# A hybrid diffusion step on one core: recurrence with two numerators, four changes of order, and weighted values on VectorE

## The reference

```python
def step(carry, inp):
    C, n, m = carry
    qb, kb, vb, ib, fb = inp
    bcum = jnp.cumsum(fb, axis=-1)
    ...
    w_inter = jnp.exp(a - m_t)
    Wd = jnp.exp(Dm - m_t[..., None])
    s = jnp.einsum('bhtd,bhsd->bhts', qb, kb) * Wd
    num = w_inter[..., None] * jnp.einsum('bhtd,bhde->bhte', qb, C) + jnp.einsum('bhts,bhse->bhte', s, vb)
    den = w_inter * jnp.einsum('bhtd,bhd->bht', qb, n) + jnp.sum(s, axis=-1)
    h = num / jnp.maximum(jnp.abs(den), jnp.exp(-m_t))[..., None]
    w_last = Wd[..., -1, :]
    wi_last = w_inter[..., -1]
    C_new = wi_last[..., None, None] * C + jnp.einsum('bhs,bhsd,bhse->bhde', w_last, kb, vb)
```

## Time and profile before

| | before |
|---|---|
| median of 3 runs | 2494.33 us (2493.68 to 2495.67) |
| the profiled execution | 2489.8 us, of which the span of the core's instructions is 2488.0 |
| TensorE busy | 2420.6 us, 97% of the span, 14856 matmuls |
| VectorE busy | 1769.2 us, 71% |
| ScalarE busy | 909.0 us, 37% |
| GpSimd busy | 347.4 us, 14% |
| DMA | 289.76 MB, 116 GB/s on the mean |
| mean granted TensorE clock | 0.996 of full speed |

### The profile page before, as it was taken

How to read it: one execution, slowest core, us unless ns; L and a number is a source line. 1 busy time by engine, 2 the same in 40 slices (tenths; PEclk the granted TensorE clock), 3 DMA queues, 4 the chain that set the end, 5 groups by cost and what they waited for, 6 DMA issues and landing times. The chain is left out here.

```text
span 2488.0 us, 38914 instructions
## 1 busy us (share of the span) xinstructions
PE 2420.6 (97%) x14856; PEld 2227.7 (90%) x14856; DVE 1769.2 (71%) x2701; ACT 909.0 (37%) x1745; POOL 347.4 (14%) x373
## 2 busy tenths in 40 slices
PE   6999999999999899999999999999999999999998
PEld 5998999789989789979988998899899979989997
DVE  4887588858454769887855988786567559856863
ACT  4211121343343554423435442343421154423432
POOL 0000000110121421202202220121200021201211
PEclk9999999999999999999999999999999999999999
DMA  6544455435222323263342326333244323243332
GB/s 241 161 143 134 129 152 163 134 111 148 72 57 73 93 98 94 64 218 100 86 154 81 88 68 212 102 86 124 80 144 136 104 83 103 69 149 98 86 125 95
DMA packets 359638, 289.76 MB, mean 116 GB/s; under 512 B 38918, under 2 KB 317334, under 8 KB 358454
## 3 DMA queue, kind: packets, MB, share of 16 engines
q1 hardware_dynamic: 359478, 287.59, 38.2%
HBM read 275.32 MB, written 12.18 MB: 116 GB/s over the span
## 5 line engine op out<-in xcount | busy, mean ns | idle before, releaser
L2031 DVE TENSOR_TENSOR w_lo<-w_raw,w_hi 128x512 fp32r<-128x512 f32 (+2 forms) x287 | 259.4, 905 | 295.9 <-ACT w_hi L1445 292.9
L1445 ACT ACTIVATE w_hi<-w_raw 128x512 fp32r<-128x512 f32 (+2 forms) x287 | 228.9, 800 | 603.4 <-PE psum L1035 213.3
L960 PE MATMUL psum<-w_hi,act_hi 128*128 128x512 f32 x800 | 319.4, 399 | 8.9 <-DVE w_lo L2031 8.7
L962 PE MATMUL psum<-w_hi,act_lo 128*128 128x512 f32 x800 | 317.2, 396 | 0.0
L961 PE MATMUL psum<-w_lo,act_hi 128*128 128x512 f32 x800 | 317.0, 396 | 0.0
L1035 PE MATMUL psum<-hT_hi,w_hi 128*128 128x320 f32 x1216 | 278.3, 310 | 0.6 <-DVE w_lo L2031 0.5
L1035 PE MATMUL psum<-hT_hi,w_lo 128*128 128x320 f32 x1216 | 277.1, 309 | 0.0
L1035 PE MATMUL psum<-hT_lo,w_hi 128*128 128x320 f32 x1216 | 276.9, 309 | 0.0
L1079 PE MATMUL psum<-hT_hi,w_hi 128*128 128x320 f32 x684 | 211.6, 309 | 1.6 <-DVE z_quarters L2314 1.6
L1080 PE MATMUL psum<-hT_lo,w_hi 128*128 128x320 f32 x684 | 211.4, 309 | 0.0
L1081 PE MATMUL psum<-hT_hi,w_lo 128*128 128x320 f32 x684 | 211.3, 309 | 0.0
(11 more groups left out here) (299 smaller groups left out, 5309.4 us busy)
## 6 DMA issues: line engine op xcount, KB each, us to landing
w_raw<-in_ffn_w_dram SPq DMA_DIRECT2D x116, 512.0 KB, 4.4
w_raw<-in_ffn_w_dram SPq DMA_DIRECT2D x148, 256.0 KB, 2.9
w_raw_next<-in_ffn_w_dram SPq DMA_DIRECT2D x60, 512.0 KB, 5.4
ada_raw<-in_ada_w_dram SPq DMA_DIRECT2D x56, 512.0 KB, 3.6
ada_tile_ffn<-in_ada_w_dram SPq DMA_DIRECT2D x40, 512.0 KB, 4.7
w_raw<-in_ab_w_in_dram SPq DMA_DIRECT2D x28, 512.0 KB, 4.2
w_raw<-in_sc_w_in_dram SPq DMA_DIRECT2D x24, 512.0 KB, 4.1
ada_first<-in_ada_w_dram SPq DMA_DIRECT2D x4, 2048.0 KB, 18.9
```

The costliest lines, as they stand in the source:

```text
L960: mm(out, a_hi, b_hi, start=first, stop=False)
L962: return mm(out, a_lo, b_hi, start=False, stop=final)
L1445: A(dst, src, ACT.Copy).then_inc(w_hi_ok, 1)
L2031: V.tensor_tensor(d_, a, b.bitcast(F32), ALU.subtract).then_inc(w_lo_ok, 1)
```

## The change

Five parts.

1. Opening: the first modulation's matmuls are run in quarters, each as soon as its piece of `ada_first` is there, three of them between the transposes; ScalarE splits the first weights ahead of copying the rows.
2. Loads of the ab input phase: the first three tiles of the modulation are placed at units 4, 4 and 5 in place of 2, one step of theirs moves from unit 8 to 7 and one from 9 to 8, and the cached keys, values and state are loaded at unit 6.
3. Output phases of the seven-product halves: the splits of unit 1's weights stand right behind those of unit 0, ahead of the last gating work, on ScalarE and VectorE.
4. Recurrence: the numerators alternate between two pairs of banks, so that `back(q)` waits for `ml_h` of step q-2; the raw scores of steps 0, 1 and 2 are copied out of PSUM by ScalarE (`keep_scores`) for steps 7, 6 and 5; `products(q + 2)` stands behind `back(q)`; ScalarE makes `w_inter` of steps 0 and 1 first, and in its loop `inter(q + 2)` stands behind `decay(q + 2)` and ahead of the squares and the splits.
5. `v_weighted` of the eight steps that need a state is multiplied by VectorE (`weigh_values`), right behind the score of the step, in place of GpSimd.

```diff
-STEPS = {"ffn": [1 + j for j in range(16)], "ab": [2, 2, 3, 3, 4, 4, 5, 5, 7, 8, 9, 9, 10, 10, 11, 11], "sc": [2 + j for j in range(16)]}
+STEPS = {"ffn": [1 + j for j in range(16)], "ab": [2, 2, 3, 3, 4, 4, 5, 5, 7, 7, 8, 9, 10, 10, 11, 11], "sc": [2 + j for j in range(16)]}
...
-FIRST_LOAD, NEXT_LOAD = 2, {"ffn": 3, "ab": 2, "sc": 2}
+FIRST_LOAD = {"ffn": (2, 2, 2), "ab": (4, 4, 5), "sc": (2, 2, 2)}
+NEXT_LOAD = {"ffn": 3, "ab": 2, "sc": 2}
...
+        Sk = [at(f"scores_kept{i}", [P, MLH, P], hl + 4096 + i * 2048) for i in range(3)]
...
-                                dma(ktok[:], cache_k[0, 0].rearrange("h p d -> p h d")).then_inc(ctx_loaded, 16)
-                                dma(vctx[:], cache_v[0, 0].rearrange("h p d -> p h d")).then_inc(ctx_loaded, 16)
...
+                            if u == 6:
+                                dma(ktok[:], cache_k[0, 0].rearrange("h p d -> p h d")).then_inc(ctx_loaded, 16)
+                                dma(vctx[:], cache_v[0, 0].rearrange("h p d -> p h d")).then_inc(ctx_loaded, 16)
...
+            def first_modulation(h):
+                pe.wait_ge(csil_ok, 1)
+                pe.wait_ge(ada_landed[h], 16)
+                for k in (2 * h, 2 * h + 1):
+                    for i in range(PRO):
+                        last = mm(PS[32 * i:32 * i + 2, i, :], csil[:, :, k], ada0[:, k, i * MODW:(i + 1) * MODW], start=(k == 0), stop=(k == KD - 1))
+                if h == KD // 2 - 1:
+                    last.then_inc(mod_mm, 1)
+
...
-            pe.wait_ge(csil_ok, 1)
-            for k in range(KD):
-                if k % 2 == 0:
-                    pe.wait_ge(ada_landed[k // 2], 16)
-                for i in range(PRO):
-                    last = mm(PS[32 * i:32 * i + 2, i, :], csil[:, :, k], ada0[:, k, i * MODW:(i + 1) * MODW], start=(k == 0), stop=(k == KD - 1))
-            last.then_inc(mod_mm, 1)
+                if t in (1, 3, 4):
+                    first_modulation((1, 3, 4).index(t))
+            first_modulation(KD // 2 - 1)
...
-                                pe.wait_ge(ml_st, 8)
+                                pe.wait_ge(ml_st, 3)
+                                pe.wait_ge(sc_kept, 3)
                             elif t < 2:
-                                pe.wait_ge(ml_h, len(ML_STEPS))
+                                pe.wait_ge(ml_h, len(ML_STEPS) - 1)
...
-                    if q == 2:
-                        pe.wait_ge(in_evac[1], ph["iv_end"][1])
+                    if q in (2, 3):
+                        pe.wait_ge(ml_st, q - 1)
+                        pe.wait_ge(sc_kept, q - 1)
...
-                    if q:
-                        pe.wait_ge(ml_h, q)
+                    if q >= 2:
+                        pe.wait_ge(ml_h, q - 1)
+                    elif q == 1:
...
-                        o_ = PS[:, 4 + h // 2, (h % 2) * 256:(h % 2) * 256 + MLD + 1]
+                        o_ = PS[:, NUM_BANK[q % 2] + h // 2, (h % 2) * 256:(h % 2) * 256 + MLD + 1]
...
+                    back(q)
                     if q + 2 in SCORE_STEPS:
                         products(q + 2)
-                    back(q)
...
+                split(plan[0][0]["nin"])
                 act.wait_ge(mod_mm, 1)
                 for i in (2, 3):
                     A(mrow0[:, i, :], PS[32 * i:32 * i + 2, i, :], ACT.Copy).then_inc(first_row, 1)
-                split(plan[0][0]["nin"])
                 split(plan[0][0]["nin"] + 1)
...
-                        split(ph["nout"], shape="out", prod=slot_done(ph, 0))
+                        for u in range(2):
+                            split(ph["nout"] + u, shape="out", u=u, prod=slot_done(ph, u))
...
-                for q, (dr, cc) in enumerate(ML_STEPS):
+                def inter(q):
+                    dr, cc = ML_STEPS[q]
                     if q >= 2:
                         act.wait_ge(ml_qs, min(q - 1, 8))
                         act.wait_ge(ml_cs, sum(1 for z in NEEDS_STATE if z < q - 1))
+                    else:
+                        act.wait_ge(m_spread[q], 16)
                     for h in range(MLH):
                         last = A(wi[:, q % 2, h, :], Mb[q][:, h, :], ACT.Exp, scale=-1.0, bias=mpb[:, h, dr, cc:cc + 1])
                     last.then_inc(ml_wi, 1)
+
+                def keep_scores(i):
+                    act.wait_ge(ml_st, i + 1)
+                    A(Sk[i][:], PS[:, SCORE_BANK[i], :].rearrange("p (h t) -> p h t", h=MLH), ACT.Copy).then_inc(sc_kept, 1)
+
+                inter(0)
+                inter(1)
+                keep_scores(0)
+                keep_scores(1)
+                for q, (dr, cc) in enumerate(ML_STEPS):
                     if q + 2 < len(ML_STEPS):
                         decay(q + 2)
+                    if q == 1:
+                        keep_scores(2)
+                    if q + 2 < len(ML_STEPS):
+                        inter(q + 2)
                     if q - 2 in whole_at:
                         head_squares(whole_at.index(q - 2))
                     if q in (1, 3, 5):
...
+                    def scaled_queries(q):
+                        cc = ML_STEPS[q][1]
+                        pool.wait_ge(ml_wi, q + 1)
+                        if q >= 2:
+                            pool.wait_ge(ml_num, q - 1)
+                        pool.tensor_tensor(qs[:, q % 2], FT[:, 8:12, cc * P:(cc + 1) * P], wi[:, q % 2], ALU.mult).then_inc(ml_qs, 1)
+
...
-                            pool.wait_ge(ml_w, q + 1)
-                            if q == 0:
-                                pool.wait_ge(tr_evac, len(TURNED))
-                            if nv >= 2:
-                                pool.wait_ge(ml_c, nv - 1)
-                            wl = Wx[q % 4][:, :, edge:edge + 1].to_broadcast([P, MLH, MLD + 1])
-                            pool.tensor_tensor(vw[:, nv % 2], vmt[:, cc], wl, ALU.mult).then_inc(ml_vw, 1)
-                            nv += 1
+                        if cc < CT and q != 1:
+                            scaled_queries(q)
                         if q == 0:
+                            scaled_queries(1)
                             masked(2)
                         if q + 3 < len(ML_STEPS):
                             masked(q + 3)
...
-                    split(ph["nout"] + u, shape="out", u=u)
+                    if u > 1 or not seven(ph):
+                        split(ph["nout"] + u, shape="out", u=u)
...
-                    V.tensor_tensor(STs[:, q % 2], PS[:, SCORE_BANK[q], :].rearrange("p (h t) -> p h t", h=MLH), Wx[q % 4][:], ALU.mult).then_inc(ml_st, 1)
+                    if q in SCORE_KEPT:
+                        dve.wait_ge(sc_kept, SCORE_KEPT[q] + 1)
+                        src = Sk[SCORE_KEPT[q]][:]
+                    else:
+                        src = PS[:, SCORE_BANK[q], :].rearrange("p (h t) -> p h t", h=MLH)
+                    V.tensor_tensor(STs[:, q % 2], src, Wx[q % 4][:], ALU.mult).then_inc(ml_st, 1)
+
+                def weigh_values(q):
+                    if q not in NEEDS_STATE:
+                        return
+                    dr, cc = ML_STEPS[q]
+                    j = NEEDS_STATE.index(q)
+                    edge = P - 1 if dr == 0 else 0
+                    if q == 0:
+                        dve.wait_ge(tr_evac, len(TURNED))
+                        dve.wait_ge(ones_ok, 2)
+                    if j >= 2:
+                        dve.wait_ge(ml_c, j - 1)
+                    wl = Wx[q % 4][:, :, edge:edge + 1].to_broadcast([P, MLH, MLD + 1])
+                    V.tensor_tensor(vw[:, j % 2], vmt[:, cc], wl, ALU.mult).then_inc(ml_vw, 1)
 
                 def finish(q):
                     dr, cc = ML_STEPS[q]
                     edge = P - 1 if dr == 0 else 0
                     dve.wait_ge(ml_num, q + 1)
-                    num = pair(4).rearrange("p a (b c) -> p (a b) c", b=2)
+                    num = pair(NUM_BANK[q % 2]).rearrange("p a (b c) -> p (a b) c", b=2)
                     dn = den[:, q % 2, :]
...
+                weigh_values(0)
                 dve.wait_ge(aT_evac, 4)
                 dve.sem_inc(act_ready, KD // 2)
                 for q in range(len(ML_STEPS)):
                     if q + 1 < len(ML_STEPS):
                         score(q + 1)
+                        weigh_values(q + 1)
...
-SCORE_BANK = [0, 1, 2, 3, 3, 2, 1, 0, 3, 3]
+SCORE_BANK = {0: 0, 1: 1, 2: 0, 3: 1, 4: 1, 8: 1, 9: 1}
+SCORE_KEPT = {5: 2, 6: 1, 7: 0}
+NUM_BANK = (4, 2)
```

23 lines of the change are left out of this document (9 added, 14 removed).

## The result

| | before | after |
|---|---|---|
| median of the runs on the same chip | 2494.88 us (10 runs, 2490.42 to 2497.44) | 2500.6 us (10 runs, 2496.9 to 2503.21) |
| ratio of after to before | | 1.0029, 95% interval 1.0021 to 1.0037 |
| the profiled execution | 2489.8, span 2488.0 | 2499.87, span 2498.1 |
| mean granted clock in it | 0.996 | 0.992 |
| TensorE busy | 2420.6 | 2425.1 |

The change makes the kernel slower by 0.29%, 7.2 us (5.2 to 9.2). The forecast was 2492.6, no change that can be measured, with a range to 2499.5; the time lies outside it.

A forecast was written before the change was run, and what follows sets the result against it. The prediction took the kernel to be bound by TensorE's work, left alone by the change, plus its idle places. Terms -1.7 - 2.2 - 2.9 + 5.1 = -1.7 on 2494.3 gave 2492.6 us, range 2485.5 to 2499.5.

The forecast's parts named there:

- Opening, -1.7: Opening: ScalarE's copies of the rows begin at 34.05 instead of 35.72, 1.7 us less, the later chain keeping its length.
- Loads, -2.2: Input phase of ab: waits of 2.9 and 0.8 go, 1.5 comes back; -2.2 us, from +1 to -3.3.
- the 1.5 us taken for the new waits at units 5 and 10: Input phase of ab: late third tile at unit 5, 0 to 2 us, and an extra step at unit 10, up to 1.
- Output phases, -2.9: Six output phases of the halves: waits before unit 1 go, partly moved to unit 2; -2.9 us, from -2 to -4.5.
- an earlier unit 1 only moves the wait: gain 0: Output phase around 1723.54: unit 2's weights are ready exactly when needed, at 1727.3, so nothing is gained.
- Recurrence, +5.1: Recurrence: +4.3 us by the layout of the engines and +0.8 for their mutual effect; +5.1, from +2 to +9.
- what the two engines do to each other: Recurrence: two new VectorE products, steps 3 and 5, start during GpSimd work and take 0.42 more each; +0.8 us.
- the 4.9 of the layout: Recurrence: VectorE's line from first denominator to last head values goes from 37.2 to 42.1 us, 4.9 later.
- (c): Recurrence rival: VectorE and GpSimd block each other over nine instructions, midway 0.85 us each; 2499.5 us, chance 0.10.
- (d): Recurrence rival: TensorE's clock falls in the 5.8 us stop before step 7; about 2497 us, chance 0.12.
- (a): Recurrence rival: ScalarE's reordered split and squares stall nobody; sum -10.6, 2483.7 us, chance 0.13.
- (b): Output phases rival: all six waits before unit 1 are won, -6.4 in place of -2.9; 2489.1 us, chance 0.13.

The follow-up runs named there:

- part_loads: Only the changed places of the loads in the ab input phase, against the kernel before: median 2492.32 us, ratio 0.9996.
- part_sevens: Only the split of unit 1 moved ahead in the six output phases of the halves, against the kernel before: median 2496.37 us, ratio 1.0020.
- rec_values_gpsimd: Only the recurrence changed, with the weighted values kept on GpSimd and ScalarE's order as changed, against the kernel before: median 2498.99 us, ratio 1.0019.
- part_opening: Only the opening's change of order, against the kernel before: median 2492.66 us, ratio 0.9997.

## Why the prediction was wrong

- **Opening, -1.7.** Right at the place: -1.74 at the first input product (-1.2 with the opening alone). In the total it is too small to be seen.
- **Loads, -2.2.** Wrong in size by the waits, though the time of part_loads would allow it. The step that failed is the 1.5 us taken for the new waits at units 5 and 10; they measure 1.79 and 0.93, with a third of 0.58 at unit 9 that I hadn't laid out. 3.7 of waits became 3.3.
- **Output phases, -2.9.** Wrong in sign, and the first of the two causes of the miss: alone +5.0. The failing step is "an earlier unit 1 only moves the wait: gain 0", with its remark that an earlier load behind unit 2 could only help. I held unit 2's landing to be fixed, or to come earlier. It isn't: the split of unit 1 also frees the buffer for unit 3, whose load then runs beside that of unit 2 and delays it by 0.6, 1.3 and 1.3 us (in the phase shown 5.6 from issue to split in place of 4.3), in three of six phases. There the waits before units 1 and 2 grew by 0.9, 1.5 and 1.2 where 0, 0 and -0.4 were laid out. The waits of 2.3 to 2.6 that come of it were followed by stretches at a lower granted clock in two of them (0.63 in 1285 to 1290, 0.68 in 1735 to 1740). In the three first halves -1.06, -0.3 and -1.06 came about as forecast, with 0.4 for the middle one. All six together are +1.2 in the waits; the rest of the +5.0 is the open part named at part_sevens.
- **Recurrence, +5.1.** Wrong in size, and the second cause: alone +9.5. The mechanism was right in each of its parts: 1.93, 1.93 and 1.92 for the splits where 2.03 were laid out, 1.85 for 1.95 at the head factor, TensorE's stop before step 7 (4.0 for 5.8). Mis-sized is "what the two engines do to each other", +0.8. I priced two of the new products at the 0.42 of one row. Lengthened were whichever of VectorE's products have both inputs in SBUF and start while GpSimd is in a 512-wide one, and the price is what is left of that one, up to 1.1 us: among the six values +0.7 in all (0.92 and 1.15 for 0.68), two low weight parts +1.3, a score from the copied values +1.1, a head's scaling +1.1. That is 4.2, less 0.5 that before had in its own low parts: +3.7 in place of +0.8. Most of it is not in the moved values, and rec_values_gpsimd keeps 3.3 of the 4.2. With the 4.9 of the layout and the 0.6 that the numerator of step 7 took longer at the low clock it is 9.2, and the window shows 9.3. The Trainium skill ("SBUF — State Buffer", § Who interferes with whom) lets a VectorE instruction with two SBUF inputs contend with a GpSimd instruction that reads SBUF, and one with at most one such input, outside the 2-port modes, not. The scores from PSUM at 0.68 and those from the copies at 1.04 on the mean in the changed kernel agree. In the kernel before, a scaling at 839.76 took 0.68 although GpSimd's factor of 4 columns ran from 839.24 to 840.25, so not every instruction of GpSimd has this price.
- **Rivals.** (c) and (d) both happened within the recurrence, beside the stalls and not in place of them: a product of the values at 1.15, and a clock of 0.50 in 840 to 845; (a), that the order of ScalarE stalls nobody, is refuted by the three waits; (b) by the waits of 2.3 to 2.6.
- **The range.** Its upper end was built on one rival at a time. Two mis-sized terms of one sign lie above it. Measured alone, the four terms miss by 14.5 us together, the whole by 8.9. Whether the parts offset each other in the whole or this is the noise of the parts, no run shows.

## What to carry to other kernels

When a split or a copy is moved ahead, follow the buffer that it frees: the load behind it starts earlier too and can delay the one that the matmul needs next. An instruction that waits for the chain must not stand in a queue ahead of work that another engine of the chain waits for; here this order alone was worth 8 us. The recurrence with a second pair of PSUM banks was a loss of 9.5 with it; the gain of 7 came when the order, the place of the values and that of the head factor were all put right. Before work is moved from GpSimd to VectorE, count every VectorE instruction with two SBUF inputs in the stretch, not only the moved ones, and look at what GpSimd is in when each of them starts.

## What the runs showed of the hardware

A VectorE product of 128x512 with both inputs in SBUF that starts with 0.2 us or more of a GpSimd product of that width still to run ends 0.54 to 0.56 us after GpSimd's. This holds for all 30 lengthened ones that can be set beside such a row of GpSimd, in the recurrence of seven traces, and gives durations of 0.74 to 1.77 in place of 0.68. With 0.12 us or less still to run they take 0.68 or 0.69. When VectorE is first, GpSimd's product is lengthened instead, from 1.27 to as much as 1.8 (1.71 at 823.88, which began while VectorE was in the low part of 823.13). A score from PSUM at 813.77, beside the same kind of GpSimd product, took 0.68.

The same wait is followed by a lower clock in one execution and not in another. In the input phase of ab TensorE waits 2.93 in the kernel before and 2.90 with the opening alone changed; the five us around and behind it are, before and in part_opening:

```profile
545.00:550.00 5.00, 3.79 (x26) 3.80 (x27) 4.90 (x6) 0.92 (x4) 0.00 (x0) 1.00 0.35 81
```

```profile
545.00:550.00 5.00, 5.00 (x19) 5.00 (x20) 4.89 (x6) 0.01 (x1) 0.00 (x0) 0.50 0.47 118
```

At 0.50 TensorE runs 19 matmuls in five us without a wait among them, where before it runs 26 with 1.2 us of the wait in the stretch. That the wait comes ahead of the lower clock in the one and not in the other, the rows show; what decides it they don't. part_sevens has a wait of 2.67 followed by 0.68 in 1285 to 1290, and one of 2.68, at 1732.91, followed by full clock:

```profile
1735.00:1740.00 5.00, 5.00 (x23) 4.03 (x22) 3.80 (x4) 1.79 (x3) 0.00 (x0) 1.00 0.74 237
```

The kernel before spreads from 2487.4 to 2499.1 us over its runs, and the mean clock of the runs goes with it, loosely: the median is 2489.7 over the 13 of the 97 runs at 0.996, 2493.3 over the 30 at 0.994, 2495.8 over the 8 at 0.992, and the slowest run has 0.993. The profiled execution of before, 2489.8, has two stretches of five us with a lower clock ahead of its last 20 us, the one of after has ten; that goes with the two traces being 10 us apart and the medians 6 to 7. So a wait of two to three us can cost more than its own length, by an amount that one profile doesn't show.
